# Recurrent stage: the second output gate product on VectorE goes behind the first recurrence, the scans of the two directions are waited for one by one, and GpSimd splits the second weight tile earlier

## The reference, cut to what matters

```python
xb, zb = jnp.split(y @ w_in, 2, axis=-1)          # 1024 -> 2048 + 2048
xb = dwconv(xb, conv_w) + conv_b                  # 4 taps
for d in range(2):                                # two directions
    gates = einsum("btnc,gncm->gbtnm", xh, gate_w[d]) + gate_b[d]
    r, i = sigmoid(gates[0]), sigmoid(gates[1])
    log_a = -8 * softplus(-lam[d]) * r
    a = exp(log_a)
    b = sqrt(-expm1(2 * log_a)) * (i * xf)
    h = linear_recurrence(a, b)                   # reversed in time for d == 1
o = (outs[0] + outs[1]) * silu(zb)
y = o @ w_out
```

## Time and profile before

| | |
|---|---|
| median of 3 runs | 3145.27 us (3144.13 to 3149.03) |
| the profiled execution, its own time | 3154.63 us |
| its span | 3152.9 us, granted clock 0.93 in the mean |
| PE busy | 2707.3 us (86%) |
| DVE busy | 1758.6 us (56%) |
| ACT busy | 1235.9 us (39%) |
| POOL busy | 1183.8 us (38%) |

### The profile page before, as it was taken

The page is one execution under the profiler, slowest core; times in us unless marked ns, Lnnn a source line. Parts: engine busy times, 40 slices in busy tenths (PEclk is TensorE's granted clock), DMA queues, the critical chain, the costliest instruction groups (busy, mean ns, idle before and its releaser), DMA issues. The chain is left out here.

```text
span 3152.9 us, 53264 instructions
## 1 busy us (share of the span) xinstructions
PE 2707.3 (86%) x18741; PEld 2594.3 (82%) x18741; DVE 1758.6 (56%) x2671; ACT 1235.9 (39%) x2107; POOL 1183.8 (38%) x1110
## 2 busy tenths in 40 slices
PE   4699999975997379999999789999999999985994
PEld 3699999975996269999999789998998999975993
DVE  3266666664300537777778646766666666654004
ACT  2255555554202224444444434454554544542001
POOL 3333333321230124444444334554444555433220
PEclk9899999987999779999999979999999999997996
DMA  3111111112413135555444451424233243214214
GB/s 111 48 54 50 51 53 48 50 36 75 149 63 139 51 73 154 148 152 153 147 144 142 117 153 44 106 55 106 76 76 106 45 115 105 47 28 159 77 47 162
DMA packets 249413, 292.60 MB, mean 93 GB/s; under 512 B 87419, under 2 KB 210892, under 8 KB 247580
## 3 DMA queue, kind: packets, MB, share of 16 engines
q1 hardware_dynamic: 244636, 273.35, 30.0%
q10 hardware_dynamic: 4608, 17.04, 1.7%
HBM read 194.30 MB, written 96.05 MB: 92 GB/s over the span
## 5 line engine op out<-in xcount | busy, mean ns | idle before, releaser
L1888 ACT ACTIVATE zz<-ps 104x416 fp32r<-104x416 f32 x560 | 286.9, 518 | 393.0 <-PE ps L1779 391.7
L543 PE MATMUL ps<-dn_yhi,dn_whi 128*128 128x416 f32 (+1 forms) x1152 | 395.2, 343 | 22.0 <-POOL dn_wlo L527 16.6
L1951 DVE TENSOR_TENSOR pp<-ps,level_mask 104x416 fp32r<-104x416 f32 x560 | 318.6, 586 | 124.4 <-PE ps L1779 123.6
L544 PE MATMUL ps<-dn_ylo,dn_whi 128*128 128x416 f32 (+1 forms) x1152 | 376.1, 326 | 0.0
L545 PE MATMUL ps<-dn_yhi,dn_wlo 128*128 128x416 f32 (+1 forms) x1152 | 375.9, 326 | 0.0
L543 PE MATMUL ps<-rg_yhi,rg_whi 128*128 128x416 f32 (+1 forms) x768 | 257.7, 336 | 82.4 <-DVE zs L829 41.7
L1781 PE MATMUL ps<-pp,zz 104*104 104x208 f32 x1440 | 267.2, 296 | 18.4 <-DVE pp L1951 16.0
L544 PE MATMUL ps<-rg_ylo,rg_whi 128*128 128x416 f32 (+1 forms) x768 | 256.8, 334 | 0.0
L545 PE MATMUL ps<-rg_yhi,rg_wlo 128*128 128x416 f32 (+1 forms) x768 | 255.8, 333 | 0.0
L1781 PE MATMUL ps<-zz,pp 104*104 104x208 f32 x1440 | 247.8, 282 | 0.0
L543 PEld LDWEIGHTS ps<-dn_yhi,dn_whi 128*128 128x128 f32 x1152 | 218.8, 190 | 28.4 <-POOL dn_wlo L527 17.0
(11 more groups left out here) (276 smaller groups left out, 7402.9 us busy)
## 6 DMA issues: line engine op xcount, KB each, us to landing
c_nq<-nq_scratch SPq DMA_DIRECT2D x160, 169.0 KB
dn_raw<-in_dn_w_in SPq DMA_DIRECT2D x48, 512.0 KB, 4.1
qd<-rows_scratch SPq DMA_DIRECT2D x160, 104.0 KB, 3.2
rg_raw<-in_rg_w_in SPq DMA_DIRECT2D x32, 512.0 KB, 3.9
nq_scratch<-p_nq SPq DMA_DIRECT2D x48, 338.0 KB
p_ex<-rows_scratch SPq DMA_DIRECT2D x32, 422.5 KB
nq_scratch<-p_rn SPq DMA_DIRECT2D x32, 338.0 KB
o_scratch<-a SPq DMA_DIRECT2D x16, 520.0 KB, 2.8
```

The lines of the kernel that those rows point to most:

```text
L543: e.matmul(o, whi, mhi[:, t0:t0 + tn], start=(first and k == 0), stop=False)
L544: e.matmul(o, whi, mlo[:, t0:t0 + tn], start=False, stop=False)
L1888: e.activation(zz[:, b, :, :], ps[0:CH, 2 * b + 1, 0:m4], ACT.Copy).then_inc(zev.sem, 1)
L1951: e.tensor_tensor(D4(pp[:, b, l % 2, :, :]), D4(Y4), c["level_mask"][:, l, :, 0:CH].unsqueeze(2).to_broadcast([CH, 2, 2, CH]), ALU.mult).t ...
```

## The change

Three edits, all in `rg_loop`.

1. DVE: `z(1)` moves from behind `recur(1)` to behind `recur(0)`.
2. ACT: the counter of the scans starts at 3 instead of 1, and q = 0 waits for two scans of the turn before (`at(n, -2)`, the backward direction) instead of four; q = 4, the first tile of the forward direction, waits for all four.
3. POOL: `lows` is cut into `low(n, t)`, and the order is x_unit 0, low 0, x_unit 1, low 1 instead of x_unit 0, low 0, low 1, x_unit 1.

```diff
-        scan, osum, odone = S("scan", 4), S("osum", 2), S("odone", 2)
+        scan, osum, odone = S("scan", 4, 3), S("osum", 2), S("odone", 2)
...
-            def lows(n):
-                for t in range(2):
-                    e.wait_ge(xhi_done.sem, xhi_done.at(n, t + 1))
...
+            def low(n, t):
+                e.wait_ge(xhi_done.sem, xhi_done.at(n, t + 1))
...
-                if more:
-                    x_unit(n + 1, 0)
-                if not last:
-                    lows(n + 1)
-                if more:
-                    x_unit(n + 1, 1)
+                for t in range(2):
+                    if more:
+                        x_unit(n + 1, t)
+                    if not last:
+                        low(n + 1, t)
...
                     if q == 0:
+                        e.wait_ge(scan.sem, scan.at(n, -2))
+                    if q == 4:
                         e.wait_ge(scan.sem, scan.at(n, 0))
-                    if q == 4:
                         for b in range(2):
                             e.wait_ge(o_out[b].sem, o_out[b].at(n, 0))
...
-                recur(0), recur(1)
+                recur(0)
                 z(1)
-                recur(2), recur(3)
+                recur(1), recur(2), recur(3)
```

More of the change, by code:

```diff
@@ L640, in x_unit @@
                 wt.split_unit(e, n, X0 + t, tile, t - 1)
-            def lows(n):
-                for t in range(2):
-                    e.wait_ge(xhi_done.sem, xhi_done.at(n, t + 1))
-                    hold(e, s.passed)
-                    e.tensor_tensor(xlo[:, t, :], xc[:, t, :], xhi[:, t, :], ALU.subtract) \
-                        .then_inc(xlo_done.sem, 1)
+            def low(n, t):
+                e.wait_ge(xhi_done.sem, xhi_done.at(n, t + 1))
+                hold(e, s.passed)
+                e.tensor_tensor(xlo[:, t, :], xc[:, t, :], xhi[:, t, :], ALU.subtract) \
+                    .then_inc(xlo_done.sem, 1)
             def turn(n, more, last):
@@ L656, in turn @@
                 wt.split_unit(e, n, Z0, tile, 4, gone=gone), wt.split_unit(e, n, Z1, tile, 8, gone=gone)
-                if more:
-                    x_unit(n + 1, 0)
-                if not last:
-                    lows(n + 1)
-                if more:
-                    x_unit(n + 1, 1)
+                for t in range(2):
[3 more added lines that the diff above has]
+                        low(n + 1, t)
             wt.split_unit(e, 0, X0 - 2, tile, -2), wt.split_unit(e, 0, X1 - 2, tile, -2)
             x_unit(0, 0), x_unit(0, 1)
-            lows(0)
+            low(0, 0), low(0, 1)
             with e.Fori(0, LAST - 1) as n:
```

## The result

The changed kernel takes 3115.55 us (median of 4 runs, 3106.55 to 3116.68) beside 3144.7 for the kernel before: a ratio of 0.9899, 95% interval 0.9873 to 0.9925, or 32 us less by the ratio (24 to 40) and 29 by the two medians. The forecast was 3103, in a range of 3086 to 3118. The direction and nearly every start and end inside a turn came as worked out; one term of the sum hardly came at all: the clock. With it gone the sum is that of rival B, 3115.

What follows compares the result with a forecast made beforehand. PE was taken to be bound by waits for z(1) before X1 and, in the last turn, for ACT's eviction. Six turns gave 34.2 us, the last turn 8.0: 42.2 off 3145.27, so 3103, range 3086 to 3118.

Steps and rivals of the forecast that it cites:

- the clock: PE behind the stall before X1: a 3.3 us stall costs no clock, so all 2.1 us a turn return, six turns.
- rival B: PE's clock falls all the same in a 3.3 us stall: gain 30 us, 3115; chance 0.18.
- What bounded the phase: PE stands 6.95 us before X1 in six turns for z(1), which waits only for its place in DVE's program.
- The price of the POOL edit: X1's split among DVE's taps of tile 1: taps end 2.7 us late, leaving 3.3 us of stall.
- rival A: The DVE-POOL collision costs little: stall at most 1.1 us, gain 57 us, 3088; chance 0.24.
- The bound "none": Lower bound for the clock behind the shorter stall before X1: none of the 2.1 us a turn comes back.
- The sign named for B: Matmuls of 0.55 us behind the stall before X1 would show that the clock falls all the same.
- The last turn: ACT's wait for scans at q = 0 goes, 10.0 us; the store delays q = 6 by 2.0; 8.0 left.
- The sum for the phase: Six turns of 3.6 us stall plus 2.1 us clock, 34.2, and 8.0 in the last turn: 42.2 us.
- Rival C: No change: waits of 6.3 us in the taps put z(1) back near 378; 3137 to 3145; chance 0.05.
- rival D: Slower: X1's weights land late, its split on POOL delays tile 1's low part and PE's gates; 3152 and up; chance 0.03.
- "Two matter": Of PE's waits in the recurrent phase two count: 43.8 us for zs of DVE, 5.2 us for ACT's eviction of a.

Runs made afterwards that it cites:

- Runs two: Only the POOL edit (X1 split in front of the low part of tile 1), against the kernel before: ratio 1.0037, stall before X1 8.95 us.
- seven: All three edits with X1's split (cast and low part) cut to 64 of 1024 columns, against the kernel before: ratio 0.9822, stall 0.61 us.
- eight: All three edits with the low part of tile 1 cut to 64 of 1040 positions, against the kernel before: ratio 0.9840, stall 1.31 us.
- run six: DVE and ACT edits with z(1) moved in front of the taps of tile 1, POOL's order as before, against the kernel before: ratio 0.9957.
- run four: DVE and ACT edits without the POOL edit, against the kernel before: ratio 0.9887, stall before X1 2.52 us.
- the run with a stall of 2.50 us: Only the DVE edit (z(1) behind recur(0)), against the kernel before: ratio 0.9902.

## Why the prediction came out as it did

- **What bounded the phase**: right. `z(1)` waited only for its place; moving it moved PE's start.
- **The price of the POOL edit**: right, and it is what kept rival A out. Forecast and measured: taps 6.7 and 6.77 us, first scan 4.6 and 4.59, stall 3.3 and 3.43. The tie between scan and low part went as in the rows before. Runs two, seven and eight show each part alone. The sentence that X1's weights would hold PE to 374 or 375 had POOL's order stayed is right too (2.5 us of stall is 374.1 in that turn's time), though it was not followed to its end: it says that the POOL edit loses.
- **The clock, the step that failed**: "3.3 is nearer to 2.14, so I take all of it". 6 x 2.1 = 12.6 us were booked; the loss went from 2.1 to 2.0 us a turn, so almost nothing came. The bound "none" was the true one, or nearly, which is rival B. The sign named for B was there too: behind four of the six stalls the first matmul took 0.67 to 0.71 us and the next 0.55. Two rows, one of which (2.14 us) was a single stall just behind a gate tile that itself ran at 0.68 of the clock, were too few to choose between the ends. The runs show that nearness in length was the wrong measure: a stall of 2.4 or 2.50 us, close to the 2.14, still costs 1.5 to 1.6, and one of 8.95 us only 2.0. Why the single stall of 2.14 us cost nothing stays open.
- **The last turn**: the ACT wait went, and the store took part of its place, as written: 1.95 us of stall before q = 6, 2.0 forecast. ACT's rows, against the earlier trace rows:

```profile
674.41 1.28 ACT L781 ACTIVATE a<-ps,gpar 128x832 f32<-128x832 f32 x2 [7.74 <-DVE u L840]
...
689.66 2.45 ACT L781 ACTIVATE a<-ps,gpar 128x832 f32<-128x832 f32 x4 [5.20 <-DMA o_scratch<-a]
```

From PE's first gate matmul to ACT's last gate eviction the turn is 7.0 us shorter. "Behind the gates everything of the last turn hangs on their end and moves with it" was wrong: in this turn `z(1)` has no stall to shorten, and in its new place DVE waits for ACT's tanh before it can go on with `recur(1)`:

```profile
720.78 2.32 DVE L840 TENSOR_TENSOR_SCAN u<-a,v 128x1040 f32<-128x1040 f32 x1
724.80 1.30 DVE L828 SCALAR_TENSOR_TENSOR zs<-zs,ps 128x832 f32<-128x832 f32 x2 [1.69 <-ACT zs L744]
```

That takes 1.9 us back (start of the last eviction to the next phase's first matmul, 59.6 us before and 61.5 now). The runs bear it out: the stretch is 61.3 to 61.6 us in every run that has `z(1)` behind `recur(0)` there, and 59.4 to 59.7 in every one that has it behind `recur(1)`. The last turn gave 5.1 us from its first matmul on, not 8.0.

- **The sum for the phase**: six stalls of 3.52 us less are 21.1, the last turn 5.1, the clock and its scatter from stall to stall the other 1.9: 28.1 us. Forecast 42.2: the clock is 10.7 too high (1.9 of 12.6), the last turn 2.9, the stalls 0.5. That the time lies in the range is owed to the range's reaching out to rival B, which had a chance of 0.18; and that it fell on B's 3115 is in part luck, since B too had the last turn 2.9 too high and the clock 1.9 too low.
- **Rival C** did not come, **rival D** neither: from the second to the seventh turn PE never waited for `rg_wlo` in the changed kernel, nor for `xlo` before the gates.
- **"Two matter"**, said of PE's waits, left out the longest, the 13.1 us before the last turn's gates. It was in both kernels alike, so the forecast did not suffer, but it is the next thing to look at.

## What to carry to other kernels

Ask of a step that is moved not only whom it frees but whom it now meets. Here GpSimd's casts and low parts took turns with the VectorE taps and scans, which read two operands from SBUF (three taps 6.77 us instead of 3.97), and left `z`, which reads one operand from PSUM, alone (1.27 us). So a GpSimd instruction has a price that depends on which VectorE instruction it falls beside, and it belongs beside one that nobody waits for. Where a product only frees PSUM banks for TensorE, try it ahead of work that TensorE does not wait for, and not in the order of the data; but see that the weights are ready by then too, for without that the move in front of the taps came out slower than the shorter one (run six against run four). And a short TensorE stall need not be cheaper in clock than a long one: bring it down to where the runs show no loss (1.3 us here), or count only its length as gained.

## What the runs showed of the hardware that was not expected

The half-speed stretch behind a recurring TensorE stall does not grow steadily with the stall. It cost nothing at 0.61 and 1.31 us, 1.6 us in three of five turns at 1.82, and 1.5 to 1.6 in all at 2.4 and 2.5; the means are 2.0 at 3.42, 2.4 at 4.71, 2.1 at 6.95 and 2.0 at 8.95, where single turns lose 1.4 to 2.9. Behind the stalls of 1.82 us, and behind many of those of 2.4 to 3.43, the first matmul still takes 0.45 to 0.47 us and the slow ones come 0.3 to 1.9 us later, so the speed of the first matmul behind a stall does not tell whether the clock will fall: that of the whole unit does (0.87 in the run with a stall of 2.50 us, by the window below).

```profile
362.74:376.24 13.50, 13.50 (x73) 13.30 (x74) 13.40 (x8) 0.00 (x0) 3.27 (x1) 0.87 0.13 39
```
